# A decoder step whose first FFN gets its input products as seven block products, with the index key pages gathered by GpSimd

## What is computed

```python
for i in range(DEPTH):                       # DEPTH = 2
    xp = xp + 0.5 * swiglu_ffn(xp, norm_ffn_a[i], w_ffn_a_in[i], w_ffn_a_out[i])
    # layer 0: sparse attention (indexer, top-k keys); layer 1: Mamba-2 SSD
    xp = xp + mixer(xp)
    xp = xp + 0.5 * swiglu_ffn(xp, norm_ffn_b[i], w_ffn_b_in[i], w_ffn_b_out[i])

def swiglu_ffn(x, g, w_in, w_out):
    h = rms_norm(x, g) @ w_in                # 1024 -> 2 * 2816
    a, b = jnp.split(h, 2, axis=-1)
    return (jax.nn.silu(a) * b) @ w_out      # 2816 -> 1024
```

## Time and profile before

| | us |
|---|---|
| median of 3 runs | 2466.77 |
| lowest and highest run | 2459.82, 2467.97 |
| span of the profiled execution | 2518.3 |
| PE busy in it | 2414.0 (96%) |
| DVE, ACT, Pool busy | 1636.9 (65%), 1019.5 (40%), 475.1 (19%) |
| mean granted TensorE clock | 0.951 |

### The profile page before, as it was taken

The page is one execution under the profiler, slowest core; times in us unless marked ns, Lnnn a source line. Parts: engine busy times, 40 slices in busy tenths (PEclk is TensorE's granted clock), DMA queues, the critical chain, the costliest instruction groups (busy, mean ns, idle before and its releaser), DMA issues.

```text
span 2518.3 us, 47284 instructions
## 1 busy us (share of the span) xinstructions
PE 2414.0 (96%) x18898; PEld 2261.8 (90%) x18898; DVE 1636.9 (65%) x2354; ACT 1019.5 (40%) x1765; POOL 475.1 (19%) x337
## 2 busy tenths in 40 slices
PE   8999999998779999999999999999999989999999
PEld 7999999767446799999999999999997779999999
DVE  5333345644364379759889669777766984795794
ACT  3221223223433345425445435432465643453452
POOL 3320333113230330000230000310285303100000
PEclk9999999957678999999999999999998989999999
DMA  4223223213233212322223222232353012122222
GB/s 162 95 87 123 94 83 111 68 69 118 68 135 135 101 67 91 104 87 105 85 86 104 100 90 95 96 144 83 117 227 150 1 51 100 68 101 101 100 89 98
DMA packets 61052, 251.23 MB, mean 100 GB/s; under 512 B 9376, under 2 KB 25888, under 8 KB 41056
## 3 DMA queue, kind: packets, MB, share of 16 engines
q1 hardware_dynamic: 56672, 223.94, 25.4%
q0 software_dynamic: 4224, 25.17, 2.9%
HBM read 233.58 MB, written 15.49 MB: 99 GB/s over the span
## 4 chain that ended last, share of the span: by engine, by line
PE 87%; DVE 5%; ACT 3%; issue 2%; another core or an unknown queue 1%; POOL 1%; DMA 0%; DVEq 0%; ACTq 0%; POOLq 0%
PE acc L702 23%; PE acc L823 23%; PE acc L672 18%; PE acc L1501 4%; PE acc L2907 3%; PE acc L1595 1%; PE acc L809 1%; PE acc L2976 1%; PE acc L1874 1%; PE acc L1910 1%; PE acc L1898 1%; ACT wh L415 1%; PE acc L3025 1%; DVE wl L474 1%
## 5 line engine op out<-in xcount | busy, mean ns | idle before, releaser
L415 ACT ACTIVATE wh<-raw 128x2048 fp32r<-128x2048 f32 x134 | 256.3, 1913 | 428.6 <-PE acc L702 321.0
L672 PE MATMUL acc<-xa,wh 128*128 128x268 f32 x2208 | 364.0, 287 | 12.4 <-DVE xa L483 12.4
L474 DVE TENSOR_TENSOR wl<-raw,wh 128x2048 fp32r<-128x2048 f32 x124 | 294.2, 2372 | 112.4 <-ACT wh L415 112.2
L823 PE MATMUL acc<-xe,wh 128*128 128x268 f32 (+1 forms) x1680 | 326.8, 286 | 0.3
L823 PE MATMUL acc<-xa,wh 128*128 128x268 f32 (+1 forms) x1680 | 326.2, 285 | 0.7 <-ACT sq L1062 0.5
L672 PEld LDWEIGHTS acc<-xa,wh 128*128 128x128 f32 x2208 | 308.7, 189 | 12.5 <-issue 12.3
L702 PE MATMUL acc<-gh,wh 128*128 128x268 f32 (+1 forms) x1408 | 288.6, 286 | 8.1 <-DVE wl L474 6.8
L702 PE MATMUL acc<-gl,wh 128*128 128x268 f32 (+1 forms) x1408 | 287.3, 285 | 0.0
L702 PE MATMUL acc<-gh,wl 128*128 128x268 f32 (+1 forms) x1408 | 287.0, 285 | 0.0
L823 PEld LDWEIGHTS acc<-xa,wh 128*128 128x128 f32 x1680 | 261.3, 188 | 1.8 <-DVE scr L1218 1.0
L823 PEld LDWEIGHTS acc<-xe,wh 128*128 128x128 f32 x1680 | 261.0, 188 | 1.1 <-DVE scr L1218 0.7
(11 more groups left out here) (553 smaller groups left out, 4625.1 us busy)
## 6 DMA issues: line engine op xcount, KB each, us to landing
raw<-in_w_ffn_in SPq DMA_DIRECT2D x88, 1024.0 KB
raw<-in_w_ffn_out SPq DMA_DIRECT2D x32, 768.0 KB
raw<-in_w_ssd_in SPq DMA_DIRECT2D x21, 1024.0 KB
raw<-in_w_ffn_out SPq DMA_DIRECT2D x32, 640.0 KB
raw<-in_w_attn_in SPq DMA_DIRECT2D x9, 1024.0 KB
kic<-in_kpages SPq DMA_DIRECT2D x64, 128.0 KB
xT<-in_state_ssm SPq DMA_DIRECT2D x8, 1024.0 KB, 7.4
out_hs<-xT SPq DMA_DIRECT2D x8, 1024.0 KB, 3.9
```

The costliest lines, as they stand in the source:

```text
L415: nc.scalar.activation(wh[:, slot], raw[:, slot], ACT.Copy).then_inc(wh_ready, 1)
L474: nc.vector.tensor_tensor(wl[:, slot], raw[:, slot], wh[:, slot].bitcast(F32), ALU.subtract).then_inc(wl_ready, 1)
L672: mm = nc.tensor.matmul(acc[:, slot * 4 + 2 * t + h, 0:(N - lo) // 2], w[:, slot, c:c + P], x[:, kt, half_of(lo, h)], start=(kt == 0 and w ...
L823: mm = nc.tensor.matmul(bank(n, number), w[:, slot, c:c + P], x_pair(f, low, i)[:, m0:m0 + hc], start=(number in (1, 2, 5) and i == 0 and ...
```

## The change

**Input chunks of FFN 0.** `in00` from its third chunk on and all of `in01`, 20 chunks in all, are formed as blocked chunks by the same code as in FFN 1 to 3. The two plain chunks of `in00` take x in pairs. FFN 0's own functions go (`act_ffn_in`, `dve_ffn_in`, `pool_ffn_in`, the loops), and its output chunks are evicted as FFN 2's are, in two DVE instructions (the products are now scaled there).

**The start.** For each pair i of tiles, ACT writes two scaled tiles (`xgain`) and then their high part, DVE the rest (128x1072), and three instructions of differences (`xmix`). The high parts and rests of the mixed operands come later. Pool squares four tiles and adds up all eight squares; ACT squares the other four.

**The index key pages.** As `kic` lies over `xe`, which FFN 0 now reads to the end of `in01`, the pages are fetched later, and by Pool: 64 indirect DMAs of 128 rows x 512 bytes, two pages each. 40 of them stand inside `pool_sumsq` of `out01`, five ahead of each tile, and 24 ahead of `pool_keys`.

```diff
@@ def _blocked():
-    for f in range(1, 4):
+    for f in range(4):
...
 def pool_sumsq(pool, chain, k, section, tiles=1):
         for n in range(DT):
+            if section == "out01":
+                pool_index_pages(pool, 5 * n, 5 * n + 5)
...
 def pe_ffn(pe, f, k):
-            if f:
-                pe_blocked(pe, f, g)
-            else:
-                pe_pairs(pe, f"in{f}{g}", lambda kt: pe.wait_ge(xl_ready, DT * k + kt + 1), norm=None if g else k)
+            pe_blocked(pe, f, g)
...
+    def act_first_pair(act, i):
+        for half in range(2):
+            t = i + 4 * half
+            act.wait_ge(x_loaded[t], 16)
+            nc.scalar.activation(xgain[:, i, half * N:(half + 1) * N], xT[:, t], ACT.Copy, scale=gains[:, 0, t:t + 1]).then_inc(x_made, 1)
+        act.wait_ge(x_made, 2 * i + 2 if i < 3 else 10)
+        nc.scalar.activation(x_pair(0, 0, i)[:, 0:2 * N], xgain[:, i], ACT.Copy).then_inc(xh_ready, 1)
...
+    def dve_first_pair(dve, chain, i):
+        dve.wait_ge(xh_ready, i + 1)
+        nc.vector.tensor_tensor(x_pair(0, 1, i)[:, 0:2 * N], xgain[:, i], x_pair(0, 0, i)[:, 0:2 * N].bitcast(F32), ALU.subtract
+                                ).then_inc(xl_ready, 1)
...
+        chain.link(nc.vector.scalar_tensor_tensor(d[1], d[0], -1.0, b[2], ALU.mult, ALU.subtract))
+        nc.vector.scalar_tensor_tensor(d[3], d[1], -1.0, b[3], ALU.mult, ALU.subtract).then_inc(x_mixed, 1)
...
+    def pool_first_squares(pool, chain):
+        for n, t in enumerate(PAIRED):
+            if n < 4:
+                pool.wait_ge(x_loaded[t], 16)
+                chain.link(nc.gpsimd.tensor_tensor(ssum[:] if n == 0 else squares[:, t], xT[:, t], xT[:, t], ALU.mult))
+            else:
+                pool.wait_ge(x_made, (7, 8, 11, 12)[n - 4])
+            if n:
+                ins = nc.gpsimd.tensor_tensor(ssum[:], ssum[:], squares[:, t], ALU.add)
...
+    def pool_index_pages(pool, first, last):
+        rows = I["kidx"].rearrange("a d c -> (a d) c")
+        for n in range(first, last):
+            u, g = n % (S // 2), n // (S // 2)
+            nc.gpsimd.indirect_dma_start(kic[:, u, g], None, rows, bass.IndirectOffsetOnAxis(irow[:, n:n + 1], 0)).then_inc(kic_loaded, 16)
...
     def pool_attention(pool, chain):
+        pool_index_pages(pool, 5 * DT, S // 2 * NPG)
         pool_keys(pool)
...
@@ def _(sp):
-                        sp_stream(sp, section, source, width, start, lambda i: sp_index_pages(sp, i + page))
...
+                for g in range(2):
+                    sp_blocked(sp, f, g)
+                    sp_out(sp, f, g)
...
@@ def _(pool):
+                if section == "out01":
+                    pool.wait_ge(rows_ready, 1)
+                    pool.wait_ge(chunk_done, BASE["out01"] + CREDIT)
                 pool_sumsq(pool, chain, n + 1, section, tiles)
```

More of the change, by code:

```diff
@@ L372, in chunks @@
                 chain.end(1)
[L375 to L405, removed]
-        else:
-            chunks(sp, count, load)
     def act_round(act, base, i, u):
@@ L484, in dve_low @@
                                        ALU.mult, ALU.subtract).then_inc(xl_ready, 1)
[L486 to L561, removed]
-                out = dst[:, ds(i * 2 + ((first + u) * 2 + t), 1)].rearrange("p a (h n) -> p (a h) n", h=2)
-                nc.vector.tensor_tensor(out, pair(slot, t), halves(rstd[:]), ALU.mult
-                                        ).then_inc(epilogue_done if t == tiles - 1 else dve_side, 1)
-        if k is None:
-            chunks(dve, count, body)
-        else:
-            body(0, 0, k)
-            body(0, 1)
-            with dve.Fori(1, count // 2) as i:
-                for u in range(2):
-                    body(i * 2, u)
@@ L576, in square @@
-    def square(t):
-        return hT[:, t]
-    def add_squares(eng, ops, chain, out, first, ready):
-        eng.wait_ge(x_squared, first + 2)
-        chain.link(ops.tensor_tensor(out[:], square(first), square(first + 1), ALU.add))
-        eng.wait_ge(x_squared, first + 3)
-        chain.link(ops.tensor_tensor(out[:], out[:], square(first + 2), ALU.add))
-        eng.wait_ge(x_squared, first + 4)
-        ops.tensor_tensor(out[:], out[:], square(first + 3), ALU.add).then_inc(ready, 1)
     def pool_sumsq(pool, chain, k, section, tiles=1):
@@ L771, in sp_blocked @@
         base, first = BASE[f"in{f}{g}"], sum(GROUPS[:g])
-        for j in range(COUNT[f"in{f}{g}"]):
+        for j in range(0 if f or g else 2, COUNT[f"in{f}{g}"]):
             n = base + j
@@ new lines, in pool_index_pages, with dve_index_rows @@
+    def pool_index_pages(pool, first, last):
[3 more added lines that the diff above has]
+            nc.gpsimd.indirect_dma_start(kic[:, u, g], None, rows, bass.IndirectOffsetOnAxis(irow[:, n:n + 1], 0)).then_inc(kic_loaded, 16)
+    def dve_index_rows(dve, chain):
+        dve.wait_ge(consts_loaded, 64)
+        for half in range(2):
+            rows = slice(half * HD, (half + 1) * HD)
+            own = pages[rows].rearrange("p (u e g) -> p e g u", e=2, g=NPG)[:, half]
+            chain.link(nc.vector.scalar_tensor_tensor(irow[rows].rearrange("p (g u) -> p g u", g=NPG), own, float(HD),
+                                                      lane[rows, 0:1].unsqueeze(2).broadcast_to([HD, NPG, S // 2]), ALU.mult, ALU.add))
+        nc.vector.tensor_scalar(irow[HD:P], irow[HD:P], float(HD), None, ALU.subtract).then_inc(rows_ready, 1)
@@ L1083, in act_blocked @@
             act_std(act, k)
+            if f == 0:
+                for i in range(1, 4):
+                    act_first_mixed(act, i)
             if f == 1:
@@ L1260, in dve_blocked @@
             plain_gate(0)
+            if f == 0:
+                for i in range(1, 4):
+                    dve_first_mixed(dve, i)
             sums_13(n0)
@@ L3712, in _ @@
         dve_rest(dve, 0, 0, 0)
-        dve.wait_ge(gains_loaded, 16)
-        for t in range(DT):
-            dve.wait_ge(x_loaded[t], 16)
-            dve_low(dve, 0, t)
-        add_squares(dve, nc.vector, chain, sq, DT // 2, sq_ready)
+        for i in range(4):
+            dve_first_pair(dve, chain, i)
+        dve_rest(dve, 1, 0, 0)
+        dve_first_mixed(dve, 0)
         for what in order:
@@ L3760, in _ @@
         pool_consts(pool, chain)
[L3761 to L3762 removed]
+        pool_first_squares(pool, chain)
         for n, what in enumerate(order):
[L3764 to L3768 removed]
             if what == "attn":
```

151 lines of the change are left out of this document (51 added, 100 removed).

## The result

The changed kernel takes 2469.68 us in the median of 20 runs (2458.83 to 2484.91), the kernel before, run beside it, 2464.44 (20 runs, 2459.77 to 2468.67). The ratio is 1.0022, with a 95% interval of 1.0012 to 1.0032: 5.4 us slower, between 3 and 8 (5.2 by the medians). 2475 was forecast, for +7.9; of the 5 us between 2475 and 2469.7, 2.3 are the lower median of the kernel before.

A forecast was written before the change was run, and what follows sets the result against it. PE was taken as the bound, busy 96% of the span. FFN 0 ends 14.4 us earlier, but a 20.9 us wait plus 1.4 makes it 7.9 us slower: 2466.8 + 7.9, rounded to 2475, range 2453 to 2488.

The forecast's parts named there:

- The block products: In FFN 0's input chunks: blocked chunks gain 12.9 us in each half, 25.8 us in all, firm to within 1 us.
- The start: At the program's start: blocked chunks begin at an effective 50.5 against 39.4, a loss of 11.1 us.
- without any turns: At the start, if DVE and Pool did not exclude each other: rests every 3.0 us, start at 42.1, loss 2.7 us.
- The turns: DVE and Pool exclude each other, the later waiting for the other's end; in out01 this adds 17.5 us, between 14 and 21.
- The index DMAs: On Pool in out01: 8.8 us of work per tile against 7.5 available; sum of squares ready 89.7 us into out01, at 422.9.
- PE's wait: At the norm's matmuls before the attention: PE waits 20.9 us for Pool's sum, and 1.4 us more is lost behind it.
- The reader of the pages: Behind the sum: the last 24 index DMAs are done at 457, hidden from their reader with some 25 us to spare.
- Rival 1: In out01: DMAs not held up by DVE, PE waits 3 to 8 us, 6.8 us faster, 2460; chance 0.18.
- rival 2: Start and out01: neither the start nor the DMAs suffer, 18.0 us faster, 2449; chance 0.14.
- rival 3: In out01: Pool slower still, PE waits 33.4 us, 12.5 us more than forecast, 2487; chance 0.16.
- The decision point: At the norm before the attention: the change is slower than before once PE's wait exceeds 13 us (14.4 less 1.4).
- the class "same": Whole kernel: a difference below about 0.3%, 7.4 us, counts as no change; chance 0.33, against slower 0.47 and faster 0.20.

The follow-up runs named there:

- e7: The changed kernel with seven of eight tiles left out of the first norm's sum, Pool squaring one and adding none: 2460.52 us, ratio 0.9975 to the kernel before.
- e3: The changed kernel with no index DMAs ahead of the sum of squares in out01 and all 64 behind it: 2477.61 us, ratio 1.0043 to the kernel before.
- e2: The changed kernel with three index DMAs ahead of each tile of out01 instead of five, 40 behind the sum: 2451.58 us, ratio 0.9925 to the kernel before.
- e4: The changed kernel with ACT making all eight first squares and PE adding them up, Pool idle at the start: 2466.89 us, ratio 1.0001 to the kernel before.
- e1: The kernel before, FFN 0 plain, with only the key pages fetched by Pool's 64 indirect DMAs as in the change: 2488.83 us, ratio 1.0090.
- e5: The changed kernel with first squares on ACT, their sum on PE, and three index DMAs a tile: 2447.63 us, ratio 0.9914 to the kernel before.
- e6: The changed kernel with three index DMAs a tile, first squares on ACT, their sum shared by Pool and PE: 2446.97 us, ratio 0.9918 to the kernel before.

## Why the prediction was right, and where its sizes were off

**The block products** were priced by FFN 2's rows and came out to a tenth: 105.6 us for `in00`'s ten chunks, 71.5 for `out00`, and the start of `out01` follows from that of the blocked chunks: 48.5 + 105.6 + 71.5 + 105.6 = 331.2, where PE's timeline has its first matmul at 331.21. This step was right.

**The start** was put at a loss of 11.1 us, and is 48.5 - 39.4 = 9.1. The cause was right: with Pool out of the way the loss is 0.4 (e7), and the bound "without any turns", 42.1, was even too dear. The turns that I played through gave the rests of the pairs at 14.9, 22.8, 29.6 and 32.6 and the sum at 27.9; DVE's and Pool's timelines in the changed kernel show 14.9, 21.7, 27.6, 30.4 and 26.1:

```profile
12.73 2.15 DVE L705 TENSOR_TENSOR xa<-xgain,xa 128x1072 fp32r<-128x1072 f32 x1
...
19.27 2.40 DVE L705 TENSOR_TENSOR xa<-xgain,xa 128x1072 fp32r<-128x1072 f32 x1
```

```profile
10.73 3.01 POOL L726 TENSOR_TENSOR squares<-xT 128x536 f32<-128x536 f32 x1
...
17.65 8.48 POOL L730 TENSOR_TENSOR ssum<-ssum,squares 128x536 f32<-128x536 f32 x5
```

A rest of 1.27 us takes 2.15 and 2.40 here, a square of 1.08 takes 3.01. What was mis-sized first is the turns: the third rest came 2.0 us earlier than I had it, and PE with it. Second, I charged each of the waits between the pairs 1.4 us for what it costs behind it, from a wait of 3.0 us. They were 1.5 and 2.7 us long, and the longer one cost 0.3 in this trace. That makes 3.1 us: chunk 0 ends at 34.8 and not at 37.9, and chunk 1 at 46.6 and not at 49.8. Third, 1.2 us came back that I had not in the sum: PE waited inside the first blocked chunks for ACT's copy of a block product out of PSUM (L949). The 1.4 is not refuted as a price, for e3 and e2 lost 1.5 and 3.1 behind the same wait; that the change's trace lost 0.3 is the draw of one execution.

**The index DMAs** were put at 89.7 us into `out01` for the sum of squares, 72.2 of it Pool's own work and 17.5 the turns. It was 417.4 - 331.2 = 86.2, so 14.0 of turns. By durations above the undisturbed ones (0.95, 1.08 and 1.34), 10.1 us lie in the index DMAs and 4.4 in the squares and additions. I had 14 if a DMA waits only where it starts under a DVE instruction, and 21 if it also holds DVE off, and took the middle. The rows say which it was. DVE and then Pool in `out01`'s second chunk:

```profile
355.14 0.72 DVE L885 SCALAR_TENSOR_TENSOR xT<-scr,xT 128x536 f32<-128x536 f32 x1
356.27 2.29 DVE L426 TENSOR_TENSOR wl<-raw,wh 128x2048 fp32r<-128x2048 f32 x1 [0.41 <-ACT wh L385]
```

```profile
355.42 1.26 POOL L741 DMA_INDIRECT kic<-in_kidx,irow  x1 [0.30 <-issue]
356.98 2.40 POOL L741 DMA_INDIRECT kic<-in_kidx,irow  x1 [0.31 <-issue]
```

The first DMA starts under L885, which ends at 355.86, and ends 0.8 us behind it. In that last part DVE's rest of weights (its second line) starts, at 356.27, and takes its usual 2.29 us: it is not held off. The second DMA starts under that rest, which ends at 358.56, and ends 0.8 us behind it too, at 359.38. So in these rows an indirect DMA waits for DVE's instruction, and DVE doesn't wait for it. Not every DVE instruction does this. The reciprocal L431, which reads one operand, runs from 420.46 to 423.96, and the index DMAs that start under it, at 421.36, 422.61 and 423.86, take 0.95, 0.94 and 0.95 us. Here the Trainium skill ("SBUF — State Buffer", section "Who interferes with whom") says that a probe showed `tensor_copy` on DVE stalling DMAs but not `tensor_tensor`, with a reason that it marks as inferred. It does not tell plain DMAs from indirect ones. The indirect ones of this kernel, which fetch row numbers from SBUF, are held up, by these rows and by the earlier trace rows. No run here shows plain ones beside them, so that it is the fetching of the row numbers that is held up is not shown.

**PE's wait** came to 17.2 us, for 20.9 predicted. It is 3.7 less, for the 3.5 less of turns and some tenths in PE's own chunks; the earlier start does not shorten it, as e4 and e7 show, since Pool's list begins with `out01`. What such a wait costs behind it was put at 1.4 us and is 2.2 over the norm's matmuls and the next twelve, with PE at the lower of its two rates (1.2 GHz). The terms together: 7.9 predicted, less 2.0 at the start, less 3.5 of turns, plus 0.8 behind the wait, is 3.2, and the trace has 3.4. That the runs, with +5.2, lie nearer to the predicted 7.9 than the trace does is no merit of the prediction.

**The reader of the pages** was called hidden with 25 us to spare: 450.9 to 481.7 is 30, and three a tile still fits. This held.

**The rivals.** Rival 1 (DMAs not held up, a wait of 3 to 8 us) and rival 2 (nothing suffers) fell with the rows above and with the wait of 17.2 (rival 2 was 18.0 us faster, and the change is slower), and rival 3 with the wait of 17.2, where it asked for 33. The decision point was a wait of 13 us. With three a tile there is none, and the same block products make the kernel faster. That the change does what it says is seen in the 105.6. As to the chances: +5.4 us is under the 7.4 that the prediction counted as the least difference, so it fell in the class "same", to which it gave 0.33, and not in "slower", to which it gave 0.47.

**What stays open.** The trace accounts for +3.4 us and the runs' medians for +5.2. The interval, 3 to 8, holds both. The kernel before was also run beside e1 to e4 (14 runs, median 2466.22) and beside e5 to e7 (19 runs, 2466.67); against these the change is 3.5 and 3.0 us slower, which is what the trace has. Runs of one kernel differ by more than that with the granted clock of the run, and no run was made that tells a further cause from it. The cause of the clock's changes in the attention is not shown, nor is that of the three pieces of the chain before. The size of the DMAs (512 bytes a row) as such was not varied.

## What to carry to other kernels

Work put ahead of a value that PE waits for is not free because its engine is idle: count one unit of it against one chunk of PE (here 5 x 1.25 + 2.6 = 8.8 us on Pool against 7.5 on PE), add the turns with the other vector engine, and where such work has two deadlines, share it out so that both fit: 3 DMAs a tile in place of 5 were worth some 18 us here, and 0 a tile lost more than 5 did. A gain that the same code shows elsewhere in the program (FFN 2) carries over to a tenth of a us, so the rows to study are those of what the change puts in its way. Where the whole effect passes through one instruction, compare the start of that instruction in two traces, and not their spans, unless their mean granted clocks agree.

## What the runs showed of the hardware

- An indirect DMA that starts under a DVE instruction with two operands in SBUF ends 0.8 us behind that instruction, and so did one that started 0.02 us ahead of it (504.37 in the earlier trace rows); a DVE instruction that starts in those 0.8 us is not slowed (rows above). Under a reciprocal, with one operand, it takes its 0.95 us.
- Behind a wait of 17.2 us PE had a granted clock of 0.50 for its first matmuls and lost 2.2 us; behind 3.0 us it lost 1.4; behind 2.7 us it lost 0.3, 1.5 or 3.1 in three traces of the same code. So a short wait has no fixed price. Behind e3's 25.0 us at the reader it lost 2.0 (1.93, 1.64 and 1.36 us for the first three groups, against 0.99, 0.94 and 0.99 later on).
- A matmul of the ones against squares in plain f32 costs 7.23 / 16 = 0.45 us for 268 columns, in two records each (32 in the chain for 16 issued). The norm's own two cost 0.90 in the chain's row of before, so the price was there to be read. The matmuls beside it take 0.124 (14.86 / 120). My 3.6 us for e4 was half of it.
- Runs of one kernel go with the mean granted clock of the run: e6 has 2435.3 at 0.975, 2447.3 at 0.966 and 2461.6 at 0.960. The clock's share of a difference can't be told from one run.
